# Keys and queries of an attention layer by token, with norms along the row and transpositions

## The reference, cut to what matters

```python
proj = h @ w_in                              # 1024 -> 4 * 2048 + 16
q, k, v, z, f_logit = split(proj)
q = rms_norm(q per head of 128, q_norm_g)    # 16 heads
k = rms_norm(k per head of 128, k_norm_g)
c = cumsum(log_sigmoid(f_logit + f_bias))    # over tokens, per head
logits = q @ k.T * 128 ** -0.5 + c[t] - c[s], -inf where s > t
o = softmax(logits) @ v
x = x + (o * silu(z)) @ w_out
```

## Time and profile before

| | |
|---|---|
| median of 3 runs | 1958.86 us (1957.92 to 1964.7) |
| profiled execution, its own time | 1957.44 us |
| its span, first to last instruction | 1955.6 us |
| mean granted TensorE clock | 0.981 |
| busy share: TensorE, VectorE, ScalarE, GpSimd | 97%, 74%, 55%, 16% |
| chain that ended last: TensorE, VectorE, ScalarE | 74%, 11%, 8% |
| attention layer | 261.8 to 602.6 us |

### The profile page before, as it was taken

How to read it: one execution, slowest core, us unless ns; L and a number is a source line. 1 busy time by engine, 2 the same in 40 slices (tenths; PEclk the granted TensorE clock), 3 DMA queues, 4 the chain that set the end, 5 groups by cost and what they waited for, 6 DMA issues and landing times.

```text
span 1955.6 us, 32679 instructions
## 1 busy us (share of the span) xinstructions
PE 1889.9 (97%) x12534; PEld 1707.9 (87%) x12534; DVE 1451.4 (74%) x2762; ACT 1067.0 (55%) x1944; POOL 314.4 (16%) x412
## 2 busy tenths in 40 slices
PE   9999999999999999999999999999999999999997
PEld 8998778877888999989987888889999898889996
DVE  8996765556777878889967687677777667687667
ACT  5886564433445444458875545555455555555554
POOL 2996000000000000039950000002000200001000
PEclk9999999989999999998999999999999999999999
DMA  6335457644446888843454464355665353445652
GB/s 212 130 130 161 152 176 255 225 141 153 140 160 194 287 297 297 296 127 119 141 162 150 158 220 120 115 177 162 233 219 179 108 157 114 142 137 184 202 193 76
DMA packets 93899, 342.23 MB, mean 175 GB/s; under 512 B 10416, under 2 KB 10672, under 8 KB 93104
## 3 DMA queue, kind: packets, MB, share of 16 engines
q1 hardware_dynamic: 93744, 340.14, 52.8%
HBM read 339.05 MB, written 1.05 MB: 174 GB/s over the span
## 4 chain that ended last, share of the span: by engine, by line
PE 74%; DVE 11%; ACT 8%; issue 5%; POOL 1%; DMA 0%; SPq 0%; DVEq 0%; ACTq 0%; POOLq 0%
PE ps L103 73%; DVE wl L119 4%; ACT tmp L109 3%; ACT wh L112 2%; POOL B L119 1%; DVE B L119 1%; PE ps L106 1%; ACT B L109 1%; DVE tmp L119 1%; DVE B L124 1%; ACT os L112 1%; DVE tmp L129 0%; DVE X L129 0%; ACT XS L112 0%; ACT ps L109 0%
## 5 line engine op out<-in xcount | busy, mean ns | idle before, releaser
L103 PE MATMUL ps<-XS,wh 128*128 128x256 f32 (+1 forms) x5008 | 927.1, 287 | 4.9 <-DVE wl L119 3.7
L103 PEld LDWEIGHTS ps<-XS,wh 128*128 128x128 f32 (+1 forms) x5008 | 790.4, 193 | 18.2 <-issue 7.5
L119 DVE TENSOR_TENSOR wl<-raw,wh 128x1024 fp32r<-128x1024 f32 (+1 forms) x489 | 595.2, 1247 | 195.5 <-ACT wh L112 195.0
L103 PE MATMUL ps<-XS,wl 128*128 128x256 f32 (+1 forms) x2504 | 711.9, 284 | 0.0
L112 ACT CAST wh<-raw 128x1024 fp32r<-128x1024 f32 (+1 forms) x489 | 489.9, 1038 | 93.6 <-PE ps L103 87.3
L103 PEld LDWEIGHTS ps<-XS,wl 128*128 128x128 f32 (+1 forms) x2504 | 482.8, 193 | 0.0
L119 POOL TENSOR_TENSOR B<-B,tmp 128x237 f32<-128x237 f32 (+11 forms) x384 | 274.4, 755 | 740.2 <-ACT tmp L109 740.2
L103 PE MATMUL ps<-wh,os 128*128 128x512 f32 x864 | 285.1, 396 | 12.5 <-DVE os L119 9.0
L129 DVE SCALAR_TENSOR_TENSOR ps<-B,C,ps 128x254 f32<-128x254 f32 (+16 forms) x544 | 211.9, 471 | 21.6 <-ACT ps L109 21.2
L103 PEld LDWEIGHTS ps<-wh,os 128*128 128x128 f32 x864 | 163.1, 189 | 51.5 <-DVE os L119 13.0
L103 PE MATMUL ps<-B,raw 128*128 128x256 f32 x832 | 194.2, 395 | 0.0
(11 more groups left out here) (154 smaller groups left out, 1795.2 us busy)
## 6 DMA issues: line engine op xcount, KB each, us to landing
raw<-in_w SPq DMA_DIRECT2D x623, 512.0 KB, 4.5
raw<-in_w SPq DMA_DIRECT2D x12, 384.0 KB, 3.7
B<-in_ln SPq DMA_DIRECT2D x4, 1024.0 KB, 6.8
C<-in_cst SPq DMA_DIRECT2D x1, 1109.5 KB, 10.0
X<-in_x SPq DMA_DIRECT2D x2, 512.0 KB, 5.4
out_x<-X SPq DMA_DIRECT2D x4, 256.0 KB, 2.5
cb<-in_cb SPq DMA_DIRECT2D x1, 512.0 KB, 13.1
raw<-in_w SPq DMA_DIRECT2D x2, 256.0 KB, 3.3
```

The source lines that it names most:

```text
L103: return NOTHING if self.e is None else self.e.matmul(*a, **k)
L119: return NOTHING if self.e is None else self.e.tensor_tensor(o, a, b, op)
```

## The change

Keys and queries are made by `token_major` as well, four heads (512 features) at a time, in three pairs of banks in turn. With the token on the partition, a head's norm is along the row: ScalarE squares 128 columns with an accumulator (8 small instructions per chunk), VectorE takes eight roots per partition and scales the chunk out of PSUM, TensorE turns it by 8 transpositions (two chunks later), and ScalarE and VectorE evacuate one bank each with the norm's gain as the scale. The 1/sqrt(128) is folded into the query gain. `squares` and `scale_qk` go.

The gate terms are split into a high and a low part on 32 partitions, so that one fp32r matmul over 384 columns adds them exactly; the causal mask is one bf16 matmul over 384 columns (the masks of the second block, made earlier now). The scores use two banks in turn. The forget logits use pieces of 32 columns (each 16 twice) and need no pick. An ada piece now follows each of the later pieces of a chunk of values and every second piece of keys and queries, and only every second z. The bias table's matmuls in the convolution layers move from p = 1 to 4 to p = 1, 2, 4, 5. The diff at its core:

```diff
-    out = [("b.f", tiles("b_w_in", 0, 4 * E - 112), "split")]
+    out = [("b.f", [("b_w_in", 0, 128 * k, 128, 4 * E, 16) for k in range(8) for _ in range(2)], "split")]
     u = iter(range(48))
 
-    def v(n):
+    def chunk(which, n, base, adas):
         for kp in range(4):
-            out.append((f"b.v{n}.{kp}", [("b_w_in", 0, 128 * k, 128, 2 * E + 512 * n, 512) for k in (2 * kp, 2 * kp + 1)],
-                        "split"))
-        out.append(ada_piece(0, next(u)))
+            out.append((f"b.{which}{n}.{kp}", [("b_w_in", 0, 128 * k, 128, base + 512 * n, 512)
+                                               for k in (2 * kp, 2 * kp + 1)], "split"))
+            if kp in adas:
+                out.append(ada_piece(0, next(u)))
 
     for n in range(3):
-        v(n)
+        chunk("v", n, 2 * E, (1, 2, 3))
     for which, base in (("k", E), ("q", 0)):
-        for i in range(0, 16, 2):
-            for n in range(2):
-                out.append((f"b.{which}{i}.{n}", tiles("b_w_in", 0, base + (i + n) * 128), "split"))
-            out.append(ada_piece(0, next(u)))
-    v(3)
-    for s in range(19):
-        if 0 <= s - 2 < 16:
-            out.append((f"b.z{s - 2}", tiles("b_w_in", 0, 3 * E + (s - 2) * 128), "split"))
-            out.append(ada_piece(0, next(u)))
-        if s >= 3:
-            out.append((f"b.o{s - 3}", [("b_w_out", 0, 128 * (s - 3), 128, 0, D)], "split"))
+        for n in range(4):
+            chunk(which, n, base, (1, 3))
+    chunk("v", 3, 2 * E, (1, 2, 3))
+    for h in range(18):
+        if h < 16:
+            out.append((f"b.z{h}", tiles("b_w_in", 0, 3 * E + h * 128), "split"))
+            if h % 2:
+                out.append(ada_piece(0, next(u)))
+        if h >= 2:
+            out.append((f"b.o{h - 2}", [("b_w_out", 0, 128 * (h - 2), 128, 0, D)], "split"))
...
-            if 1 <= p < 5:
+            if p in (1, 2, 4, 5):
...
-            if p in (2, 4):
-                self.act_bias(act, (4 if j else 1) + (p == 4), 3)
+            if p in (2, 5):
+                self.act_bias(act, (4 if j else 1) + (p == 5), 3)
...
+    def b_chunk(self, j):
+
+        return ((4, 5), (6, 7), (2, 3))[j % 3]
+
+    def b_norm(self, j):
+
+        a = 32 + 32 * (j % 2)
+        return [self.m["sm"][:, a + 8 * k:a + 8 * k + 8] for k in range(4)]
+
+    def b_scaled(self, j, tb):
+        return self.tmp[2 * (j % 3) + tb]
+
+    def b_turned(self, j):
+
+        K, Q, V, I16 = self.b_views()
+        X, n = (K, j - 3) if j < 7 else (Q, j - 7)
+        return [X[:, 4 * n + 2 * x:4 * n + 2 * x + 2, :].rearrange("p a t -> p (a t)") for x in range(2)]
+
+    def b_gain(self, j):
+        return self.c("b_k_norm") if j < 7 else self.m["sm"][:, 96:97]
...
-        self.unit(pe, self.ps[4][:, 0:T], "b.f", "b")
-        pe.wait_ge(*s["evac"]["b", "f"])
-        pe.matmul(self.ps[2][0:16, 0:T], self.c("ident", 112, 16), self.tmp[0][:, 0:T], start=True,
-                  stop=True).then_inc(s["small"].up("b.f"), 1)
+        self.unit(pe, self.ps[6][0:32, 0:T], "b.f", "b", 32)
...
+        def turn(j):
+            for tb in range(2):
+                pe.wait_ge(*s["evacd"]["b", "scaled", j, tb])
+            if j > 3:
+                pe.wait_ge(*s["evac"]["b", "turned", j - 1])
+                pe.wait_ge(*s["evacd"]["b", "turned", j - 1])
+            for h in range(4):
+                for tb in range(2):
+                    a = (h % 2) * T + tb * 128
+                    ins = pe.transpose(self.ps[h // 2][:, a:a + 128], self.b_scaled(j, tb)[:, 128 * h:128 * h + 128],
+                                       self.c("ident", 0, 128))
+            ins.then_inc(s["turn"].up(("b", "chunk", j)), 1)
+
+        for j in range(3, 12):
+            if j < 6:
+                pe.wait_ge(*s["evacd"]["b", "v", j - 3])
+                pe.wait_ge(*s["evac"]["b", "v", j - 3])
             else:
+                for tb in range(2):
+                    pe.wait_ge(*s["evacd"]["b", "scaled", j - 3, tb])
+            self.token_major(pe, self.b_chunk(j), "b.v3" if j == 11 else f"b.k{j - 3}" if j < 7 else f"b.q{j - 7}", "b")
+            if j >= 5:
+                turn(j - 2)
...
+            b = self.ps[4 + h % 2]
+            causal, chosen, idn = self.m_masks()
+            if h % 4 == 0:
+                pe.wait_ge(*s["evac"]["b", "turned", 7 + h // 4])
+            if h % 4 == 2:
+                pe.wait_ge(*s["evacd"]["b", "turned", 7 + h // 4])
+            pe.wait_ge(*(s["evacd"]["b", "scaled", 9, h] if h < 2 else s["exps"]["b", h - 2]))
+            pe.wait_ge(*s["soft"]["b", "terms"])
+            pe.wait_ge(*s["evac"]["choice"])
+            pe.wait_ge(*s["evac"]["masks"])
+            pe.matmul(b[:, 0:384], choice[:, h:h + 1].to_broadcast([32, 128]), terms, start=True, stop=False)
+            pe.matmul(b[:, 0:384], idn, causal, start=False, stop=False)
+            pe.matmul(b[:, 0:128], Q[:, h, 0:128], K[:, h, 0:128], start=False, stop=False)
+            pe.matmul(b[:, 128:384], Q[:, h, 128:256], K[:, h, :], start=False, stop=True).then_inc(
+                s["score"].up(("b", h)), 1)
...
+        for st in range(17):
             if st < 16:
+                scores(st)
+            if st == 0:
+                turn(10)
+            h = st - 1
+            if h >= 0:
                 if h < 2:
+                    pe.wait_ge(*s["evacd"]["b", "scaled", 10, h])
                 else:
                     pe.wait_ge(*s["soft"]["b", "o", h - 2])
+                self.unit(pe, self.ps[6 + h % 2][:, T:2 * T], f"b.z{h}", "b")
                 if h:
                     pe.wait_ge(*s["soft"]["b", "o", h - 1])
+                else:
+                    pe.wait_ge(*s["evacd"]["b", "scaled", 10, 1])
+                self.pe_turn(pe, self.tmp[h % 3], 7 - h % 2, ("b", h))
+                if h == 2:
+                    pe.wait_ge(*s["evac"]["b", "turned", 10])
+                    pe.wait_ge(*s["evacd"]["b", "turned", 10])
+                    pe.wait_ge(*s["evac"]["b", "v", 3])
+                    pe.wait_ge(*s["evacd"]["b", "v", 3])
+                if h >= 2:
+                    self.pe_out(pe, "b", h - 2, 16)
                 self.pe_value(pe, V[:, 0, h * 128:h * 128 + 128], V[:, 1, h * 128:h * 128 + 128], self.tmp[h % 3],
                               6 + h % 2, slice(0, 128), ("b", h))
+        self.pe_out(pe, "b", 14, 16)
...
+        def squares(j, tb):
+            which, n = ("k", j - 3) if j < 7 else ("q", j - 7)
+            ss, b, junk = self.b_norm(j)[0], self.ps[self.b_chunk(j)[tb]], self.b_scaled(j, tb)
+            act.wait_ge(*s["gemm"][f"b.{which}{n}", 3])
+            if j < 6:
+                act.wait_ge(*s["soft"]["b", "terms"])
+            else:
+                act.wait_ge(*s["turn"]["b", "chunk", j - 3])
+            if j > 4:
+                act.wait_ge(*s["norm"][("b", j - 2), "v"])
+            for h in range(4):
+                ins = act.activation(junk[:, 128 * h:128 * h + 128], b[:, 128 * h:128 * h + 128], ACT.Square,
+                                     accum_out=ss[:, 4 * tb + h:4 * tb + h + 1])
+            ins.then_inc(s["square"].up(("b", j, tb)), 1)
+
+        def turned(j):
+            act.wait_ge(*s["turn"]["b", "chunk", j])
+            if j >= 7:
+                act.wait_ge(*s["soft"]["b", "gain"])
+            act.activation(self.b_turned(j)[0], self.ps[0], ACT.Identity, scale=self.b_gain(j)).then_inc(
+                s["evac"].up(("b", "turned", j)), 1)
...
+        def scaled(j):
+            ss, v, d, r = self.b_norm(j)
+            for tb in range(2):
+                dve.wait_ge(*s["square"]["b", j, tb])
+            dve.ts(v, ss, 1.0 / 128, 1e-6, ALU.mult, ALU.add).then_inc(s["norm"].up((("b", j), "v")), 1)
+            self.dve_root(dve, r, v, d, ("b", j))
+            dve.wait_ge(*s["norm"][("b", j), "root"])
+            for tb in range(2):
+                dve.tt(self.b_scaled(j, tb)[:].rearrange("p (h d) -> p h d", h=4),
+                       self.ps[self.b_chunk(j)[tb]].rearrange("p (h d) -> p h d", h=4),
+                       r[:, 4 * tb:4 * tb + 4].unsqueeze(2).to_broadcast([128, 4, 128]), ALU.mult).then_inc(
+                           s["evacd"].up(("b", "scaled", j, tb)), 1)
+
+        def turned(j):
+            dve.wait_ge(*s["turn"]["b", "chunk", j])
+            dve.ts(self.b_turned(j)[1], self.ps[1], self.b_gain(j), None, ALU.mult, None).then_inc(
+                s["evacd"].up(("b", "turned", j)), 1)
...
+        dve.wait_ge(*s["soft"]["b", "ncs"])
+        dve.tensor_copy(terms[:, 128:384], ncs).then_inc(s["soft"].up(("b", "upper")), 1)
+        dve.wait_ge(*s["soft"]["b", "upper"])
+        upper, minus = terms[:, 128:384].bitcast(F32), self.c("minus", 0, 1, rows=slice(0, 32))
+        dve.stt(terms[:, 0:128], upper[:, 0:128], minus, ncs[:, 0:128], ALU.mult, ALU.add).then_inc(
+            s["soft"].up(("b", "first")), 1)
+        dve.wait_ge(*s["soft"]["b", "first"])
```

(54 more changed lines are left out.)

193 lines of the change are left out of this document (64 added, 129 removed).

## The result

| | before | after |
|---|---|---|
| median | 1959.29 us (4 runs, 1957.92 to 1964.7) | 1889.64 us (4 runs, 1887.73 to 1895.05) |
| profiled execution, its own time | 1957.44 us | 1889.36 us |
| its span | 1955.6 us | 1887.5 us |
| granted TensorE clock | 0.981 | 0.985 |

The ratio of after to before is 0.9653, 95% interval 0.9635 to 0.9671: faster by 3.5%. The forecast was 1893 us (1880 to 1914).

A forecast was written before the change was run, and what follows sets the result against it. TensorE was taken to bound the attention layer as long as VectorE keeps up. The terms 15.7 + 49.6 + 0.9 - 4.4 + 3 = 64.8 brought 1957.4 to 1893 us, range 1880 to 1914.

The forecast's parts named there:

- TensorE bounds the layer: Attention layer: time is worth what TensorE's instructions are worth, as long as VectorE keeps up; TensorE busy 97% of the span.
- Keys and queries, -15.7: Keys and queries in the attention layer: 8 chunks of 11.01 + 0.95, 95.7 us against 111.4.
- Turnings cost the clock: Rival, keys and queries: each of the 8 sets of transpositions brings a clock drop, +27, time 1920; chance 0.09.
- Scores 1.0, and VectorE nearly tied, 7.9 a head: Head loop: TensorE needs 6.62 + 1.0 = 7.6, VectorE 7.5; 7.9 taken instead of 10.40, bounds 7.6 and 8.7.
- 10.7 of VectorE's time: Chunks of keys and queries: VectorE's work per chunk was put at about 10.7 of the 11.96 us period.
- One of my own signs of failure: Heads: the forecast would be wrong if VectorE's busy share stayed under 80% with TensorE still waiting.
- Edges of the heads, 3.6: Entry and end of the head loop: edges cost 3.6 us instead of 13.2; with the heads 130.0, -49.6.
- Gate terms: Start of the attention layer: pick gone, -0.9; late split makes TensorE wait 2.7 plus 1.7 of lower clock, +4.4.
- The three values chunks with 7 pieces each: Values chunks: 7 pieces in 11 us instead of 5, 334 GB/s, priced at 0; 5 us if not so.
- Bias, -3: Bias table, both convolution layers: TensorE's 1.83 wait goes, clock losses stay; -3 for both, bounds 0 and -14.

## Why the prediction was right

The time came as forecast, 1889.64 against 1893, and so did the mechanism in the main: TensorE bounds the layer, and work taken from it comes out as time. Three of the steps came out by luck or otherwise than written, the period of the heads above all. In all, 64.8 us are gained between the forget logits and the layer's last product; the steps sum to 61.8. Point by point:

**TensorE bounds the layer: right.** It is busy for the whole of the chunks and heads, and added TensorE time in the heads came out whole (six score matmuls, 1.25 a head).

**Keys and queries, -15.7: -17.0.** A chunk is 10.92 (forecast 11.01) and a turning 0.88 (0.95), period 11.80 for 11.96; 8 x 11.80 = 94.4 against 111.4. The last values chunk brings the 0.5 that make up -17.5. Of the 1.0 per chunk between two pairs of units and a token-major chunk, the width is 0.58; the rest is put down to the form of the unit, which no run tested. The Trainium skill, "TensorE: Matmul & The Clock Gate", section "Back-to-back issue gap", would have given the width almost nothing; the same section also quotes about 131 ns as the sustained spacing at 512 columns. Neither agrees with these rows: 227 ns at 512 columns and 120 at 256, in the four-byte fast format with a weight load before each.

**Turnings cost the clock: no.** The clock is 1.00 over the 96 us that hold six of them. The Trainium skill, same page, section "Part 4: PE-mode transpose", says that transposing doesn't count as busy for the clock in the same way. By the row of windows above, 0.88 us of it between 10.9 us of dense work cost no clock here. That is no test of longer strings of them.

**Scores 1.0, and VectorE nearly tied, 7.9 a head: the period right, by two errors that cancel.** The price of the scores was read from start to start (0.83 and 0.17). That reading is met, 1.01. But the period moves by 1.29, since the products around them get longer by the other 0.28 when the scores stand between them; TensorE's need is 7.90, not 7.6. The other error was VectorE's need. I took 7.5, from the 10.40 less the two waits that I saw in the earlier trace rows; the table by stretch of the same loop has VectorE busy for only 14.61 of 20.80 us, 7.3 a head, with 1.7 more of idle time in gaps that I counted as work. Those gaps, and the 0.59 that I called a wait for the value product, are put down to ScalarE by the trace (0.98, 0.47, 0.19 and 0.59, around 500 to 510 us), and only the 0.81 to TensorE, so VectorE's waits were not "mostly for TensorE" either. Less the scalings and half a modulation row that is 5.8; measured are 6.2 (78% of 7.90). The tie that I saw did not exist, and that 7.9 came out is luck: by TensorE's 7.6 alone the sum would have been 16 x 0.3 = 4.8 us lower, 1888.

```profile
462.00:482.80 20.80, 20.80 (x120) 16.82 (x119) 14.61 (x33) 8.14 (x19) 0.00 (x0) 1.00 0.45 153
```

The chunks were given 10.7 of VectorE's time; they have 78.69 / 96 x 11.80 = 9.7. Here the instructions were priced by their own length: from start to start a split takes 1.14 instead of 1.2, and the scaling of a whole chunk 1.21 instead of 1.6. One of my own signs of failure was VectorE under 80% in the heads with TensorE still waiting: the first half came, the second didn't.

**Edges of the heads, 3.6.** 129.8 - 126.4 = 3.4, with the last transpositions taken out; I had counted those 0.95 twice, in the chunks and here. The composition was not what I wrote. The wait before the last output product went, and the low clock at the entry (0.65 before) too, 1.00 now. In their place stand waits of 1.83 and 1.22 us for the first two heads' turned probabilities, forecast as twice 0.6:

```profile
413.15 0.92 PE L103 MATMUL ps<-tmp,B 128*128 128x256 f32 x4 [1.83 <-ACT tmp L109]
419.78 0.92 PE L103 MATMUL ps<-tmp,B 128*128 128x256 f32 x4 [1.22 <-ACT tmp L109]
```

The first of them carried a table load of 1.28, which I had not seen; the early table took 1.15 back. The Trainium skill, "ScalarE: Activation LUTs", section "What ACT_TABLE_LOAD costs", gives 1283 ns for the load, and the row at 406.92 agrees with it.

**Gate terms: the wait 2.91 for 2.7, at 270.49 us for "near 270"; the clock's part 1.8 for 1.7.** This was the most exact step: it was worked out from the order of VectorE's queue. The net of the stretch is +2.5 against +3.5: the pick and the narrower unit gave 1.3 instead of 0.9, and a wait of 0.79 for VectorE at the end of the values in before (at 300.17), which I had not counted, is gone. The three values chunks with 7 pieces each brought no wait for a transfer, as priced.

**Bias, -3: not settled.** The wait of 1.83 went. Contrary to what I wrote, the clock losses did not all stay: over 74 to 112 us they halved, from 6.8 to 3.4. More than half of what was won in the first convolution layer is swallowed before its end, as I had allowed for (2.9 us at the statistics, 1.2 at the start of the attention layer, in the kernel before with this edit alone). The other 1 to 2 us at the start of the attention layer come and go between traces of the same code in that place.

**Not forecast.** The transpositions that open the next layer wait 1.55 for ScalarE, where they had waited 0.18: the layer's end got tighter, and 1.4 us were given back there.

## What to carry to other kernels

Where an engine is said to be nearly the bound, take its busy time from the table by stretch, not from the period less the waits that one has noticed. Price a small matmul between others by the period with and without it, since the distance to its neighbour hides what it does to them (1.01 against 1.29 here). When instructions are added to a queue whose look-ahead counts pieces, count again what still stands ahead of them: the wait can be forecast to some tenths of a microsecond, and splitting one piece earlier together with moving two low-priority pieces out of the way removed it.

## What the runs showed of the hardware

- An fp32r matmul of 32 rows, 384 columns and a stationary operand broadcast along its free dimension costs 0.37 us to the next start in either place, a bf16 one of 128 rows and 384 columns 0.17, and 0.26 directly behind the fp32 value product. Whether it is the type, the 32 rows or the broadcast that doubles it stays open.
- Around the 2.91 of idle time at 270 us and the 3.02 at 74 the clock fell (0.91 over 20 us, 0.51 over 8). Behind the 1.95 at 427.86 (modulation rows in the heads) it fell too (0.50 from 428 to 430), and behind the 1.83 at 73.89 in before (0.58 over 8); with the 1.91 at 274 (in the run with the splits ahead) and the 1.83 at 413 it stayed at 1.00. So the length of the last wait alone doesn't say whether the clock falls.
- The clock also fell with no wait near: behind the group of bias matmuls and single-column sums at 93.51 in before it was 0.57 from 96 to 104 us, with TensorE busy since 73.89. Behind the same group at 95.02, in the run with the bias table put back, it stayed at 1.00. What decides between the two stays open.
- 96 us of dense fp32r chunks with a set of 8 fp32 transpositions every 11.8 us kept a granted clock of 1.00.
